# Down projections by a seven-product block algorithm, with VectorE making the low part of the four-block weight sum

## The chip, the cores and the metric

One core of a Trainium2 chip runs the program. The metric is the device time of one execution in microseconds (us). TensorE multiplies, VectorE, ScalarE and GpSimd do the elementwise work, and SyncE's queue issues most DMAs. A profile of one execution gives each instruction's start and duration.

## The reference, cut to what matters

Two decoder layers on 256 tokens with a model width of 2048: a sliding-window attention layer, then a forgetting-attention layer, each followed by this feed-forward network of inner width 5632 (float32 throughout):

```
def swiglu_ffn(h, w_gate_up, w_down):
    gu = h @ w_gate_up
    gate, up = gu[..., :D_FF], gu[..., D_FF:]
    return (jax.nn.silu(gate) * up) @ w_down

# around it, for each layer i
    h = rmsnorm(x, g[2])
    y = swiglu_ffn(h, ffn_w_gate_up[i], ffn_w_down[i])
    x = x + rmsnorm(y, g[3])
```

## The kernel before, in words

The program is a row of units. A unit is 16 weight tiles of 128 rows by 512 columns, each multiplied with two blocks of 128 tokens (t = 0 and 1), so 32 steps. To keep float32 precision on a cheaper format, each weight tile and each activation tile is split into a high part and a low part, and a step is three matmuls (`product`): high by high, high activation by low weight, low activation by high weight. So a unit is 96 matmuls of 128x512.

The feed-forward network of a layer has 11 groups of 512 inner columns. Before the change a group is three units: gate, up, and down. The gate unit is read by ScalarE with a SiLU into `h_sb` (L747); VectorE multiplies it with the up result (L1061), turns it in 32x32 blocks into `h_t` (L1087, 32 instructions a group), and it is split into `h_hi` (ScalarE, L752) and `h_lo` (VectorE, L1069). The down unit multiplies it with 16 tiles of `ffn_w_down` (4 inner blocks by 4 output chunks of 512), and VectorE adds each of the 8 results to `y_sb` (`add_y`, L1106).

Weight tiles come in pairs by DMA into `stage` (8 tiles). ScalarE rounds each to `ring_hi` (`round_tile`, L607 with a gain for gate and up, L605 for down), VectorE subtracts to get `ring_lo` (`rest_tile`, L817 and L815). The ring has 24 places; `tile_used` frees them, `lo_ready` lets TensorE go on. Each engine has one queue in program order, written out by hand as steps: in step s VectorE does what the tables name for it, then one tile. GpSimd does next to nothing in the feed-forward networks: it takes two square roots per norm (L1205) and loads gains (L1274). It is at work in the attention parts: rotary (L1220 to L1226) in the first, the bias (L1265 to L1267) and its DMAs in the second. Nine of the eleven groups of each layer run in a loop of three units.

Of the kernel before, what the change touches and what calls it, by code (L numbers as in the profile page):

```python
# [43 lines left out]
LT = LOOP_UNITS * UT  # L44
# [6 lines left out]
U_FOX = U_FFN[0] + 3 * FG  # L51
U_FOX_OUT = U_FOX + FOX_UNITS
U_FFN[1] = U_FOX_OUT + NC_D
U_END = U_FFN[1] + 3 * FG
# [45 lines left out]
HIDDEN_TURNED = {(1, 17): (0, 0), (1, 19): (0, 1), (2, 1): (1, 0), (2, 3): (1, 1)}  # L100
HIDDEN_HI = {(1, 25): 0, (2, 5): 1}
HIDDEN_LO = {(1, 23): 0, (2, 5): 1}
# [32 lines left out]
def step_order(s, first=False):  # L135

    if first:
        return s // 4 % 2, s // 8 * 4 + s % 4
    return s // UT, s % UT

# [22 lines left out]
def build(nc, x, positions, norm_gains, swa_w_in, swa_sinks, swa_w_out,  # L163
          fox_w_in, fox_b_f, fox_w_out, ffn_w_gate_up, ffn_w_down, out):
    with ExitStack() as ctx:
# [40 lines left out]
        arena = sb("arena", [P, 51 * 1024 // 4])  # L206
# [22 lines left out]
        diag = at("diag", 40 * KB, [P, P])  # L229
        ssq_end = at("ssq_end", 41 * KB, [P, NC_D + 1])  # L230
# [18 lines left out]
        x_ps = [bank[b] for b in (6, 7, 4, 5)]  # L249

# [20 lines left out]
        x_sum = sem("x_sum")  # L271
        x_squared, pre_mean, pre_rstd = sem("x_squared"), sem("pre_mean"), sem("pre_rstd")
# [12 lines left out]

        cum_dram = nc.dram_tensor("cum_scratch", (NH, SEQ), F32, kind="Internal").ap()
# [4 lines left out]
        def weights(u, i, pr):  # L291
# [16 lines left out]
            if u < U_FOX or u >= U_FFN[1]:  # L308
                layer = 0 if u < U_FOX else 1
                g, part = divmod(u - U_FFN[layer], 3)  # L310
                g = g + i
                if part < 2:
                    return cols(ffn_w_gate_up[layer], g * CH + part * D_FF)
# [14 lines left out]
        def gain_row(u):  # L328
# [37 lines left out]

        def whole_program(loop, unit):

            def looped(u, n):
                with loop(n) as i:  # L370
                    for part in range(LOOP_UNITS):
# [6 lines left out]
            straight(U_SWA, U_FFN[0] + 3)  # L378
            looped(U_FFN[0] + 3, FG - 2)
            straight(U_FOX - 3, U_FOX + 3)  # L380
            looped(U_FOX + 3, NG - 2)
            straight(U_FOX_OUT - 3, U_FFN[1] + 3)
            looped(U_FFN[1] + 3, FG - 2)
            straight(U_END - 3, U_END)

        def ffn_part(u):

            for layer in range(2):
                if U_FFN[layer] <= u < U_FFN[layer] + 3 * FG:
                    return (layer, *divmod(u - U_FFN[layer], 3))  # L390
            return None
# [133 lines left out]
        def _(sp):  # L525
# [1062 lines left out]
```

## Time and profile before

| | us |
|---|---|
| median of 2 runs | 2106.19 (2106.15 to 2106.24) |
| span of the profiled execution, first to last instruction | 2104.5 |
| TensorE busy | 2094.2 |
| TensorE weight loads busy (beside the matmuls) | 1718.9 |
| VectorE busy | 1615.4 |
| ScalarE busy | 1152.9 |
| GpSimd busy | 156.6 |

The page gives the time of the execution only as its span; what lies around it is the 1.7 us between the span and the median. Busy time counts a moment once even if two pipelined instructions overlap in it, so the mean duration of one matmul (0.39 us) is longer than the distance from one to the next.

### The profile page before, as it was taken

How to read it: one execution, taken by the hardware profiler on the slowest of the kernel's cores; microseconds unless marked ns; L12 is line 12 of the kernel's file. 1: busy time of each engine (PE TensorE's matmuls, PEld its weight loads, DVE VectorE, ACT ScalarE, POOL GpSimd, SP SyncE). 2: the span in 40 equal slices, each digit the busy share in tenths (PEclk: the TensorE clock that was granted, in tenths of full speed). 3: DMA queues.
4: the chain of work that ended last, by engine and by line, in shares of the span. 5: the costliest groups of instructions: out<-in, count | busy, mean ns of one | idle time of the engine just before them, and what ended most of it. 6: DMA issues, size and time to landing. Idle time of an engine off the chain costs nothing.

```text
span 2104.5 us, 32177 instructions
## 1 busy us (share of the span) xinstructions
PE 2094.2 (100%) x9603; PEld 1718.9 (82%) x9603; DVE 1615.4 (77%) x3299; ACT 1152.9 (55%) x2061; POOL 156.6 (7%) x311
## 2 busy tenths in 40 slices
PE   9999999999999999999999999999999999999998
PEld 7877888888888888888888887888888888888886
DVE  6798677887667776678898898577877668776686
ACT  7666565544455454555666555665544545445553
POOL 2110000000000000000152343000000000000000
PEclk9999999999999999999999999999999999999999
DMA  7699866665666655665687787756555665556662
GB/s 257 211 247 253 223 206 206 195 191 173 199 199 199 197 171 190 199 204 161 202 247 219 214 251 215 234 190 216 189 187 178 199 217 184 188 178 203 206 193 87
DMA packets 221564, 425.01 MB, mean 202 GB/s; under 512 B 15808, under 2 KB 25440, under 8 KB 220976
## 3 DMA queue, kind: packets, MB, share of 16 engines
q1 hardware_dynamic: 214528, 402.45, 61.6%
q0 software_dynamic: 6672, 21.31, 3.7%
q8 instruction: 37, 0.61, 0.1%
q10 hardware_dynamic: 288, 0.33, 0.1%
q14 instruction: 39, 0.32, 0.1%
HBM read 409.31 MB, written 14.71 MB: 201 GB/s over the span
## 4 chain that ended last, share of the span: by engine, by line
PE 97%; DMA 1%; issue 1%; SPq 1%; ACT 0%; POOL 0%; DVE 0%; POOLq 0%
PE bank L1338 31%; PE bank L1340 31%; PE bank L1339 31%; PE bank L1385 1%; PE bank L1410 1%; PE bank L1351 1%; DMA x_sb<-x 0%; DMA p_f<-first_scratch 0%; DMA stage<-swa_w_out 0%; PE bank L1368 0%; SPq L541 0%; SPq L566 0%; PE bank L1432 0%; PE bank L1429 0%; PE bank L1571 0%
## 5 line engine op out<-in xcount | busy, mean ns | idle before, releaser
L1338 PE MATMUL bank<-ring_hi,a_hi 128*128 128x512 f32 x2240 | 880.3, 393 | 0.5 <-DVE ring_lo L817 0.5
L1340 PE MATMUL bank<-ring_hi,a_lo 128*128 128x512 f32 x2240 | 873.1, 390 | 0.0
L1339 PE MATMUL bank<-ring_lo,a_hi 128*128 128x512 f32 x2240 | 872.8, 390 | 0.0
L607 ACT ACTIVATE ring_hi<-stage,g_t 128x512 fp32r<-128x512 f32 x992 | 661.2, 717 | 376.6 <-DMA stage<-ffn_w_gate_up 203.0
L817 DVE SCALAR_TENSOR_TENSOR ring_lo<-stage,g_t,ring_hi 128x512 fp32r<-128x512 f32 x992 | 708.5, 759 | 147.3 <-ACT ring_hi L607 144.9
L1338 PEld LDWEIGHTS bank<-ring_hi,a_hi 128*128 128x128 f32 x2240 | 420.9, 188 | 92.9 <-issue 5.9
L1340 PEld LDWEIGHTS bank<-ring_hi,a_lo 128*128 128x128 f32 x2240 | 420.8, 188 | 88.1
L1339 PEld LDWEIGHTS bank<-ring_lo,a_hi 128*128 128x128 f32 x2240 | 421.1, 188 | 84.7
L815 DVE TENSOR_TENSOR ring_lo<-stage,ring_hi 128x512 fp32r<-128x512 f32 x480 | 305.5, 687 | 139.9 <-ACT ring_hi L605 138.5
L605 ACT ACTIVATE ring_hi<-stage 128x512 fp32r<-128x512 f32 x480 | 278.4, 624 | 225.0 <-PE bank L1340 149.5
L1338 PE MATMUL bank<-ring_hi,h_hi 128*128 128x512 f32 x704 | 274.6, 390 | 0.0
L1340 PE MATMUL bank<-ring_hi,h_lo 128*128 128x512 f32 x704 | 274.2, 389 | 0.0
L1339 PE MATMUL bank<-ring_lo,h_hi 128*128 128x512 f32 x704 | 274.2, 389 | 0.0
L1087 DVE STREAM_TRANSPOSE h_t<-h_sb 32x128 f32<-32x128 f32 x672 | 203.5, 303 | 10.8
L1340 PEld LDWEIGHTS bank<-ring_hi,h_lo 128*128 128x128 f32 x704 | 132.2, 188 | 27.4
L1338 PEld LDWEIGHTS bank<-ring_hi,h_hi 128*128 128x128 f32 x704 | 132.3, 188 | 27.2
L1339 PEld LDWEIGHTS bank<-ring_lo,h_hi 128*128 128x128 f32 x704 | 132.3, 188 | 27.1
L1205 POOL TENSOR_TENSOR post_r<-post_ms,half_pow 128x1 f32<-128x1 f32 x8 | 7.6, 948 | 1491.6 <-DVE post_ms L844 1491.6
L1106 DVE TENSOR_TENSOR y_sb<-bank,y_sb 128x512 f32<-128x512 f32 x159 | 109.5, 688 | 11.6 <-PE bank L1340 10.8
L1061 DVE SCALAR_TENSOR_TENSOR h_sb<-bank,pre_r,h_sb 128x512 f32<-128x512 f32 x44 | 33.0, 749 | 108.8 <-PE bank L1340 108.8
L752 ACT ACTIVATE h_hi<-h_t 128x512 fp32r<-128x512 f32 x42 | 26.6, 633 | 125.7 <-DVE h_t L1087 125.7
L667 ACT ACTIVATE prob<-prob,neg_mx 128x129 f32<-128x129 f32 (+3 forms) x128 | 56.9, 447 | 39.6 <-DVE neg_mx L933 39.3
(148 smaller groups left out, 836.6 us busy)
## 6 DMA issues: line engine op xcount, KB each, us to landing
stage<-ffn_w_gate_up SPq DMA_DIRECT2D x352, 512.0 KB, 4.6
stage<-ffn_w_down SPq DMA_DIRECT2D x176, 512.0 KB, 5.5
stage<-fox_w_in SPq DMA_DIRECT2D x96, 512.0 KB, 4.7
stage<-swa_w_in SPq DMA_DIRECT2D x48, 512.0 KB, 4.7
stage<-swa_w_out SPq DMA_DIRECT2D x64, 256.0 KB, 6.2
stage<-fox_w_out SPq DMA_DIRECT2D x32, 512.0 KB, 5.5
first_scratch<-first_blocks SPq DMA_DIRECT2D x16, 384.0 KB, 5.4
p_f<-first_scratch SPq DMA_DIRECT2D x64, 96.0 KB, 3.9
```

The costliest lines, as they stand in the source:

```text
L605: nc.scalar.activation(ring_hi[:, n % RING, :], src, ACT.Identity).then_inc(hi_ready, 1)
L607: nc.scalar.activation(ring_hi[:, n % RING, :], src, ACT.Identity, scale=g_t[:, row * KT + j:row * KT + j + 1]).then_inc(hi_ready, 1)
L667: last = nc.scalar.activation(prob[:, b, cols], prob[:, b, cols], ACT.Exp, bias=neg_mx[:, j, t:t + 1], accum_out=den[:, j, t:t + 1])
L752: nc.scalar.activation(h_hi[:, :, tok(t)], hidden_transposed(g, t), ACT.Identity).then_inc(ht_hi, 1)
L815: nc.vector.tensor_tensor(lo, src, hi, ALU.subtract).then_inc(lo_ready, 1)
L817: nc.vector.scalar_tensor_tensor(out=lo, in0=src, scalar=g_t[:, row * KT + j:row * KT + j + 1], in1=hi, op0=ALU.mult, op1=ALU.subtract).th ...
L1061: nc.vector.scalar_tensor_tensor(out=h_sb[:, t, :], in0=main[2 + t][:, :], scalar=pre_r[:, t:t + 1], in1=h_sb[:, t, :], op0=ALU.mult, op1= ...
L1087: last = nc.vector.transpose(h_t[Q * b:Q * (b + 1), :, P * t + Q * a:P * t + Q * (a + 1)], src)
L1106: nc.vector.tensor_tensor(dst, main[n][:, :], dst, ALU.add).then_inc(y_added, 1)
L1338: nc.tensor.matmul(dst, hi_a, hi_w, start=start, stop=False)
L1339: nc.tensor.matmul(dst, hi_a, lo_w, start=False, stop=False)
L1340: return nc.tensor.matmul(dst, lo_a, hi_w, start=False, stop=stop)
```

## The change

The down projection of the first ten of a layer's eleven groups is no longer a unit of its own. Its 4 inner blocks by 4 output chunks are taken as two halves ("pairs", of 1024 output columns each). In a half the product is one of 2x2 blocks: rows are the two token blocks, the inner dimension is two times 256, the columns two chunks of 512. A seven-product algorithm (Strassen's, in Winograd's form) makes it from 7 block products where the plain one has 8. One block product is 6 matmuls (two inner blocks by three).

- A feed-forward group is now two units, gate and up (`FFN_LOOP_UNITS = 4` for two groups). While the units of group g run, the 7 products of each half of group g-1 are put between their steps (`down_pair`, at the steps of `PRODUCT_STEPS`). Gate and up take tiles in fours, alternating between the token blocks. The eleventh group keeps its plain down unit.
- The weights of a half come by 4 DMAs of 512 KB (`load_down`) into `down_w`, which lies over `x_sb`. So `x_sb` is written to DRAM at the start of each feed-forward network (`save_x`) and read back at its end (`load_x`), both on GpSimd's queue.
- GpSimd makes four sums of weight blocks of 128x1024 for each half (`sum_weights`): T1 = B11 + B12, T3 = B22 + B12, T2 = T1 + B22, T4 = T2 + B21, and, once a group, four sums of 128x256 of the turned hidden block (`sum_hidden`). It also makes the low part of T1 (`rest(T1)`).
- ScalarE rounds the seven 128x1024 weight operands of a half (`round_pair`). VectorE makes the low parts of the other six (`rest_pair`), T4's among them: the table `POOL_LO = (T1,)` sets which of them GpSimd makes. VectorE also does the low parts of the hidden sums (`sum_rests`) and adds the seven results to `y_sb` (`add_pair`).
- The turning into 32x32 blocks takes both token blocks at once: 16 instructions of 32x256 a group for 32 of 32x128.

```diff
-LT = LOOP_UNITS * UT
+FFN_LOOP_UNITS = 4
+FFN_UNITS = 2 * FG + 1
...
+B11, B21, T1, T2, B22, T3, T4 = range(NPROD)
+POOL_LO = (T1,)
+DVE_LO = tuple(k for k in range(NPROD) if k not in POOL_LO)
+SUMS = (T1, T3, T2, T4)
...
+            def rest_pair(u, i, k):
+
+                p = NPROD * pair_number(u) + k
+                dve.wait_ge(pair_hi, p + 1 + 4 * NPROD * i)
+                both = slice(PLACE["pair", p], PLACE["pair", p] + 2)
+                if k == B22:
+                    dve.wait_ge(sums_made, 4 * pair_number(u) + SUMS.index(T4) + 1 + 16 * i)
+                nc.vector.tensor_tensor(ring_lo[:, both, :], pair_source(k), ring_hi[:, both, :].bitcast(F32), ALU.subtract).then_inc(pair_lo, 1)
...
+                wait_loaded(0)
+                if q > 0:
+                    wait_rested(T4, q - 1)
+                nc.gpsimd.tensor_tensor(sums[0][:, :, :], b11, b12, ALU.add).then_inc(sums_made, 1)
+                wait_loaded(2)
+                pool.wait_ge(pair_lo, rested + DVE_LO.index(B11) + 1)
+                nc.gpsimd.tensor_tensor(sums[1][:, :, :], b22, b12, ALU.add).then_inc(sums_made, 1)
+                pool.wait_ge(sums_made, made + 1)
+                nc.gpsimd.tensor_tensor(sums[2][:, :, :], sums[0][:, :, :], b22, ALU.add).then_inc(sums_made, 1)
+                rest(T1)
+                pool.wait_ge(sums_made, made + 3)
+                wait_rested(T1, q)
+                nc.gpsimd.tensor_tensor(sums[0][:, :, :], sums[2][:, :, :], b21, ALU.add).then_inc(sums_made, 1)
+                if q % 2 == 0:
+                    sum_hidden(q, i)
+                rest(T4)
...
+                for r in range(2):
+                    if k in (0, 1, 6):
+                        first, t = ((0, 0), (2, 0), None, None, None, None, (2, 1))[k]
+                        a_h, a_l = h_hi[:, first + r, tok(t)], h_lo[:, first + r, tok(t)]
+                    else:
+                        n = (None, None, 0, 1, 2, 3, None)[k]
+                        a_h, a_l = s_hi[:, n, r, :], s_lo[:, n, r, :]
+                    slot = PLACE["pair", p] + r
+                    last = product(ps[:, :], a_h, a_l, ring_hi[:, slot, :], ring_lo[:, slot, :], k < 3 and r == 0, r == 1, True)
+                last.then_inc(pair_done, 1)
```

How the queues change. On GpSimd, before the change, the rows of the first feed-forward network are a load of gains and the norm's powers, and nothing else:

```order
L1205 TENSOR_TENSOR pre_r<-pre_ms,half_pow 128x1 x2
L1274 DMA g_b<-norm_gains 128x2048
L1205 TENSOR_TENSOR post_r<-post_ms,half_pow 128x1
L1298 DMA fg_raw<-fox_w_in 128x16x32
L1205 TENSOR_TENSOR post_r<-post_ms,half_pow 128x1
```

After it, at the same place, `x_sb` is saved and the first half of the first group follows (sums_67 holds T1 and later T4, sums_68 holds T3, sums_69 holds T2):

```order
L1562 DMA x_scratch<-x_sb 128x2x2048
L1596 TENSOR_TENSOR sums_67<-down_w 128x1024
L1599 TENSOR_TENSOR sums_68<-down_w 128x1024
L1601 TENSOR_TENSOR sums_69<-sums_67,down_w 128x1024
L1590 TENSOR_TENSOR ring_lo<-sums_67,ring_hi 128x1024
L1605 TENSOR_TENSOR sums_67<-sums_69,down_w 128x1024
L1616 TENSOR_TENSOR s_sb<-h_t 128x256
L1618 TENSOR_TENSOR s_sb<-s_sb,h_t 128x256
L1620 TENSOR_TENSOR s_sb<-s_sb,h_t 128x256
L1621 TENSOR_TENSOR s_sb<-h_t 128x256
```

Five instructions of 128x1024 for each half and four of 128x256 for each group have come in. On VectorE, in the first group's down unit before the change, one result is added between every two tiles:

```order
L1103 COPY y_sb<-bank 128x512
L817 SCALAR_TENSOR_TENSOR ring_lo<-stage,g_t,ring_hi 128x512 x2
L1103 COPY y_sb<-bank 128x512
L817 SCALAR_TENSOR_TENSOR ring_lo<-stage,g_t,ring_hi 128x512 x2
L1103 COPY y_sb<-bank 128x512
```

After it, in the unit that holds the first half's products, an instruction of twice the width stands in nearly every place between a tile and an addition (the second row of 128x1024 below, from sums_67, is the low part of T4):

```order
L1060 TENSOR_TENSOR s_lo<-s_sb,s_hi 128x512
L1024 SCALAR_TENSOR_TENSOR ring_lo<-stage,g_t,ring_hi 128x512
L1085 TENSOR_TENSOR y_sb<-bank,y_sb 128x512
L1034 TENSOR_TENSOR ring_lo<-sums_68,ring_hi 128x1024
L1024 SCALAR_TENSOR_TENSOR ring_lo<-stage,g_t,ring_hi 128x512
L1076 COPY y_sb<-bank 128x512
L1034 TENSOR_TENSOR ring_lo<-sums_67,ring_hi 128x1024
L1024 SCALAR_TENSOR_TENSOR ring_lo<-stage,g_t,ring_hi 128x512
L1074 TENSOR_SCALAR y_sb<-bank 128x512
L1034 TENSOR_TENSOR ring_lo<-down_w,ring_hi 128x1024
L1024 SCALAR_TENSOR_TENSOR ring_lo<-stage,g_t,ring_hi 128x512
```

What moved: the low parts of the down weights were 16 rows of 128x512 a group and are now 12 rows of 128x1024, spread between the gate and up tiles.

## Rows read from the trace of the kernel before

**Rows 1.** The page: busy time by engine, slices of the span, DMA.
```profile
PE 2094.2 (100%) x9603; PEld 1718.9 (82%) x9603; DVE 1615.4 (77%) x3299; ACT 1152.9 (55%) x2061; POOL 156.6 (7%) x311
...
PE   9999999999999999999999999999999999999998
...
PEclk9999999999999999999999999999999999999999
...
HBM read 409.31 MB, written 14.71 MB: 201 GB/s over the span
```
**Rows 2.** The page: the chain that ended last, by engine.
```profile
PE 97%; DMA 1%; issue 1%; SPq 1%; ACT 0%; POOL 0%; DVE 0%; POOLq 0%
```
**Rows 3.** Timeline of TensorE (start, duration): a down unit's first, the next unit's first.
```profile
703.17 0.39 PE L1338 MATMUL bank<-ring_hi,h_hi 128*128 128x512 f32 x1
703.40 0.39 PE L1339 MATMUL bank<-ring_lo,h_hi 128*128 128x512 f32 x1
...
724.94 0.39 PE L1338 MATMUL bank<-ring_hi,a_hi 128*128 128x512 f32 x1
```
**Rows 4.** Windows: stretch, its length, busy of PE, PEld, DVE, ACT, POOL, clock, DMA.
```profile
703.17:768.44 65.27, 65.27 (x289) 54.09 (x288) 48.97 (x93) 32.86 (x52) 0.00 (x0) 1.00 0.61 193
```
**Rows 5.** Groups of VectorE instructions in 703 to 768 us: busy, mean; idle before.
```profile
L817 DVE SCALAR_TENSOR_TENSOR ring_lo<-stage,g_t,ring_hi 128x512 fp32r<-128x512 f32 x32 | 22.5, 749 | 5.4 <-ACT ring_hi L607 5.4
L815 DVE TENSOR_TENSOR ring_lo<-stage,ring_hi 128x512 fp32r<-128x512 f32 x17 | 10.8, 687 | 4.6 <-ACT ring_hi L605 4.6
...
L1106 DVE TENSOR_TENSOR y_sb<-bank,y_sb 128x512 f32<-128x512 f32 x8 | 5.5, 690 | 0.5 <-PE bank L1340 0.5
L1061 DVE SCALAR_TENSOR_TENSOR h_sb<-bank,pre_r,h_sb 128x512 f32<-128x512 f32 x2 | 1.5, 748 | 5.3 <-PE bank L1340 5.3
```
**Rows 6.** Timeline of VectorE: stretches of equal instructions back to back.
```profile
1154.45 5.35 DVE L817 SCALAR_TENSOR_TENSOR ring_lo<-stage,g_t,ring_hi 128x512 fp32r<-128x512 f32 x8
1163.21 1.77 DVE L877 STREAM_TRANSPOSE k_t<-stg 32x256 f32<-32x256 f32 x4
748.21 4.30 DVE L815 TENSOR_TENSOR ring_lo<-stage,ring_hi 128x512 fp32r<-128x512 f32 x7 [3.86 <-ACT ring_hi L605]
703.91 0.74 DVE L1061 SCALAR_TENSOR_TENSOR h_sb<-bank,pre_r,h_sb 128x512 f32<-128x512 f32 x1
704.69 2.51 DVE L1087 STREAM_TRANSPOSE h_t<-h_sb 32x128 f32<-32x128 f32 x8
```
**Rows 7.** Groups of the whole span: the same operation at two widths.
```profile
L1106 DVE TENSOR_TENSOR y_sb<-bank,y_sb 128x512 f32<-128x512 f32 x159 | 109.5, 688 | 11.6 <-PE bank L1340 10.8
L1100 DVE TENSOR_TENSOR y_sb<-bank,y_sb 128x256 f32<-128x256 f32 x2 | 0.8, 419 | 0.3 <-PE bank L1340 0.3
```
**Rows 8.** Timeline of GpSimd in the attention parts.
```profile
80.75 0.32 POOL L1221 TENSOR_TENSOR rope_tmp<-stg,rope_s 128x64 f32<-128x64 f32 x1
81.14 0.96 POOL L1224 TENSOR_TENSOR stg<-stg,rope_c 128x128 f32<-128x128 f32 x1
1164.45 0.47 POOL L1265 TENSOR_TENSOR prob<-cum_b,mask 128x128 f32<-128x128 f32 x1
1171.34 0.47 POOL L1265 TENSOR_TENSOR prob<-cum_b,mask 128x128 f32<-128x128 f32 x1
1204.68 0.46 POOL L1267 TENSOR_TENSOR prob<-cum_b,mask 128x128 f32<-128x128 f32 x1
```
**Rows 9.** Timeline of VectorE beside them.
```profile
71.58 0.74 DVE L817 SCALAR_TENSOR_TENSOR ring_lo<-stage,g_t,ring_hi 128x512 fp32r<-128x512 f32 x1
81.70 0.96 DVE L817 SCALAR_TENSOR_TENSOR ring_lo<-stage,g_t,ring_hi 128x512 fp32r<-128x512 f32 x1
1171.33 1.27 DVE L817 SCALAR_TENSOR_TENSOR ring_lo<-stage,g_t,ring_hi 128x512 fp32r<-128x512 f32 x1
1195.16 0.17 DVE L933 TENSOR_SCALAR neg_mx<-row_mx 128x2 f32<-128x2 f32 x1
1204.70 0.47 DVE L933 TENSOR_SCALAR neg_mx<-row_mx 128x2 f32<-128x2 f32 x1
```
**Rows 10.** Groups of the whole span: ScalarE's rounding of a tile, with and without a gain.
```profile
L607 ACT ACTIVATE ring_hi<-stage,g_t 128x512 fp32r<-128x512 f32 x992 | 661.2, 717 | 376.6 <-DMA stage<-ffn_w_gate_up 203.0 <-PE bank L1340 107.6 <-DMA stage<-fox_w_in 55.5
L605 ACT ACTIVATE ring_hi<-stage 128x512 fp32r<-128x512 f32 x480 | 278.4, 624 | 225.0 <-PE bank L1340 149.5 <-DMA stage<-swa_w_out 35.2 <-DMA stage<-fox_w_out 23.5
```

More of the change, by code:

```diff
@@ L132, with ffn_index, pair_unit, pair_number @@
 OUT_GAIN = {84: (0, 0), 88: (1, 0), 92: (0, 1), 98: (1, 1), 102: (0, 2), 106: (1, 2)}
-def step_order(s, first=False):
-    if first:
+def ffn_index(u):
+    for layer in range(2):
+        if U_FFN[layer] <= u < U_FFN[layer] + FFN_UNITS:
+            return layer, u - U_FFN[layer]
+    return None
+def pair_unit(u):
+    f = ffn_index(u)
+    return f is not None and 2 <= f[1] < 2 * FG
+def pair_number(u):
+    layer, n = ffn_index(u)
+    return NP_LAYER * layer + n - 2
+def in_fours(u):
+    f = ffn_index(u)
+    return f is not None and 1 <= f[1] < 2 * FG - 1
@@ new lines, in tiles_rested @@
+def tiles_rested(u, s):
+    f = ffn_index(u)
+    uneven = f is not None and f[1] > 0
+    before = ffn_index(u - 1) if u else None
+    uneven_before = before is not None and 0 < before[1] < 2 * FG
+    if s == 0:
+        if u == 0:
+            return []
+        return tiles_rounded(u - 1, STEPS - 1) if uneven_before else [(u, UT - 1)]
+    if uneven and f[1] < 2 * FG:
+        return tiles_rounded(u, s - 1)
+    if uneven and s == 1:
+        return [(u, 15)]
+    return [(u + 1, s // 2 - 1)] if s % 2 == 0 else []
@@ new lines, in pairs_rounded, with ring_places @@
+def pairs_rounded(u, s):
+    f = ffn_index(u)
+    if f is None or f[1] == 0 or s not in PAIR_HI[f[1] % 2]:
+        return []
+    later, k = PAIR_HI[f[1] % 2][s]
+    return [(u + later, k)] if pair_unit(u + later) else []
+def ring_places():
+    place, before, last = {}, {}, {}
+    n = 0
+    for u in range(U_END):
+        f = ffn_index(u)
+        fixed = f is not None and f[1] >= 2
+        if fixed and f[1] == 2:
+            first = n % RING
+        for j in range(UT):
+            slot = (first + j) % RING if fixed else n % RING
+            if not fixed:
+                n += 1
+            place[u, j] = slot
+            before[u, j] = last.get(slot)
+            last[slot] = ("tile", u * UT + j)
+        if pair_unit(u):
+            for k in range(NPROD):
+                p = NPROD * pair_number(u) + k
+                slot = (first + UT + 2 * (p % 4)) % RING
+                place["pair", p] = slot
+                before["pair", p] = last[slot + 1]
+                last[slot] = last[slot + 1] = ("pair", p)
+        if fixed and f[1] == 2 * FG:
+            n = first + UT
+    return place, before
@@ L229, in build @@
         diag = at("diag", 40 * KB, [P, P])
+        sums = [at(f"sums{n}", (32 + 4 * n) * KB, [P, 2, CH]) for n in range(3)]
+        s_hi = at("s_hi", 44 * KB, [P, 4, 2, P], F32R)
+        s_lo = at("s_lo", 48 * KB, [P, 4, 2, P], F32R)
+        s_sb = at("s_sb", 8 * KB, [P, 4, 2, P])
+        x_base = x_sb.manual_sbuf_range[0] if x_sb.manual_sbuf_range else nc.lookup_mloc(x_sb).addr
+        down_w = nc.alloc_sbuf_tensor_at("down_w", [P, 8, CH], F32, offset=x_base)
         ssq_end = at("ssq_end", 41 * KB, [P, NC_D + 1])
@@ new lines, in hidden_rests, with sum_rests @@
+            def hidden_rests(u, i):
+                layer, g, _ = ffn_part(u)
+                dve.wait_ge(ht_hi, hidden_split(layer, g - 1, 0) + 2 * i)
+                nc.vector.tensor_tensor(h_lo[:, :, :], h_t[:, :, :], h_hi[:, :, :].bitcast(F32), ALU.subtract).then_inc(ht_lo, 1)
+            def sum_rests(u, i, half):
+                dve.wait_ge(s_hi_made, pair_number(u) + half + 1 + 4 * i)
+                part = slice(2 * half, 2 * half + 2)
+                nc.vector.tensor_tensor(s_lo[:, part], s_sb[:, part], s_hi[:, part].bitcast(F32), ALU.subtract).then_inc(s_lo_made, 1)
@@ L1483, in accumulator @@
                         if g > 0:
[L1484 removed]
+                            pe.wait_ge((gate_read, hidden)[part], 2 * (f - 1) + t + 1 + 4 * i)
                         elif part == 0:
```

372 lines of the change are left out of this document (292 added, 80 removed).

## The prediction

> **What bounds the kernel now.** I read the page's busy shares first: TensorE is busy for all of the span, at full clock in every slice, VectorE for 77% [rows 1]. The chain that ended last is 97% TensorE [rows 2], so a matmul saved is time saved, as long as no other engine takes over. The price of a matmul is its distance to the next, not its duration: a down unit starts at 703.17 and the next unit at 724.94, 96 matmuls in 21.77 us, 0.227 us each [rows 3]. One feed-forward group, three such units, lasts 65.27 us; in it VectorE is busy for 48.97 us, ScalarE for 32.86 us and GpSimd not at all [rows 4]. VectorE has 16 us to spare, which is little beside what the change gives it.
>
> **TensorE.** A group's down projection goes from 96 matmuls to 2 halves x 7 products x 6 = 84. With 10 groups in each of 2 layers that is 20 x 12 = 240 matmuls, 240 x 0.227 = 54.4 us. By TensorE alone a group would last 65.3 - 2.7 = 62.6 us, and the kernel 2106.2 - 54.4 = 2051.8 us. (The sum is made against the profiled execution, whose span is 1.7 us below the median; I add the same 1.7 us behind every sum by starting from 2106.2.)
>
> **VectorE's own work.** I again take distances, of equal instructions back to back [rows 6]: a gate or up tile (5.35 - 0.75)/7 = 0.66 us, a plain 128x512 subtraction (4.30 - 0.69)/6 = 0.60 us, a narrow block transpose 2.51/8 = 0.31 us, a wide one 1.77/4 = 0.44 us, the gate multiply 704.69 - 703.91 = 0.78 us. By these a group before costs 32 x 0.66 + 16 x 0.60 + 8 x 0.60 (additions) + 32 x 0.31 + 2 x 0.78 + 2 x 0.60 = about 48 us, which agrees with the 48.97 us. No row shows a 128x1024 subtraction. At least it is one of 128x512 (0.60 us), at most two (1.20 us). From 256 to 512 columns the same operation grows from 419 to 688 ns [rows 7], 1.05 ns a column, so I take 0.60 + 0.54 = 1.14 us. A group afterwards: 32 tiles 21.1, 12 wide low parts 13.7, 14 additions 8.4, 16 wide transposes 7.1, gate multiplies 1.6, `h_lo` 1.1, `s_lo` 2 x 0.6 = 1.2: together 54.2 us. That is under 62.6, and alone it would let TensorE stay the bound. The two low parts of T4 that stand here and not on GpSimd are 2.3 us of it.
>
> **ScalarE** has 14 roundings of 128x1024 for 16 of 128x512. A narrow one takes 0.62 us [rows 10], so a wide one is between that and 1.25 us; even at 1.25 us the group costs 32.9 + 14 x 1.25 - 16 x 0.62 = 40 us of 62, hidden. I cost it at nothing. The DMAs move the same weight bytes at about 200 GB/s [rows 1]; `x_sb` is saved and read back twice, 2.1 MB each time, 10 us each at that rate. The load is issued when the last half's low parts are made, in the middle of the last up unit, and is first needed at step 17 of the last down unit, more than 25 us later; the save has the unit and a half of gate and up before SyncE's queue reaches the first `load_down`, behind which the tiles of gate and up queue. I cost them at nothing; if that cover is gone it is 10 us at each of four places.
>
> **GpSimd, and what it does to VectorE.** This decides. Per group GpSimd gets ten additions or subtractions of 128x1024 and four of 128x256. The undisturbed rows are 0.32 us at 64 columns and 0.47 us at 128 [rows 8]: 0.15 us for 64 columns, 2.27 ns a column. So 1024 columns are 0.47 + 2.03 = 2.5 us and 256 are 0.75 us, together 28 us of a group. The bound above is eight times the 128-column row, 3.8 us; the bound below is the slope of VectorE, 0.47 + 0.94 = 1.4 us. I keep 2.5, from two rows of the same engine and operation (at 3.8 a group would gain another 14 us, at 1.4 lose 12; the lower end is in the first rival, the upper in the last). In throughput 28 us would fit into 62. But the trace shows that it isn't laid beside VectorE's work. The tile at 71.58 takes 0.74 us with no addition of GpSimd at its start; the one at 1171.33 takes 1.27 us, and GpSimd's addition at 1171.34 lasts 0.47 us: the whole of it has been added. The one at 81.70 takes 0.96 us beside GpSimd's at 81.14, which itself takes 0.96 us for 0.47, since it had to wait for the tile before. A tiny VectorE instruction at 1204.70 takes 0.47 us for 0.17, until GpSimd's of 1204.68 ends [rows 8, 9]. Whoever comes second waits for the other's end. The block transposes at 1163.21 keep their 0.44 us with GpSimd's addition at 1164.45 in the middle of them [rows 6, 8], so work with one input in SBUF is spared.
>
> The Trainium skill's page "SBUF — State Buffer", section "Who interferes with whom", has this as a rule: a VectorE instruction with two SBUF inputs and a GpSimd instruction that reads SBUF share a read port, and the later one is blocked for the whole of the other. By that rule the blocking lasts the full length of a wide GpSimd addition, which no row here can show, since the widest of them is 128 columns. The same skill's "GPSIMD Engine Reference", section "Performance versus the Vector engine", gives 4497 ns at 2048 columns, by which 1024 would be an estimated 2.25 us and the sum below about 50 us smaller.
>
> What is exposed: VectorE's tiles, wide low parts, `h_lo` and `s_lo` (21.1 + 13.7 + 1.1 + 1.2 = 37.1 us) read two SBUF inputs. Additions, transposes and gate multiplies (8.4 + 7.1 + 1.6 = 17.1 us) are spared. With GpSimd's 28 that makes 65.1 us that cannot overlap, already more than TensorE's 62.6. To reach even that, all 17.1 us of spared work would have to lie under GpSimd's. It does not: in VectorE's queue a single addition of 0.60 us stands between exposed instructions, so a GpSimd addition of 2.5 us covers one of them at best. Half of the ten long ones covering one is 3 us; another 5 us I allow for time in which VectorE would wait for ScalarE or TensorE anyway (15 us a group now, [rows 5], most of which the fuller queue eats up). So VectorE needs 54.2 + 28 - 8 = 74.2 us a group. TensorE waits for it through `lo_ready`, `pair_lo` and `pair_added`; ScalarE waits behind TensorE for ring places. The sum: (74.2 - 65.3) x 20 = +178 us, 2106.2 + 178 = 2284 us. VectorE is then what is late next, and GpSimd, at 28 us plus its own waits, is not.
>
> **The rivals.**
> - TensorE stays the bound, faster: GpSimd's long additions do not hold up VectorE for their whole length (or cost near the lower bound: 10 x 1.4 + 4 x 0.6 = 16.4, less 8, makes 62.6 us, just the point at which TensorE decides). For it speaks that each engine alone fits into 62.6 us and that no row shows a wide addition; against it that every short collision in rows 8 and 9 costs the full remainder. 2052 us, up to 2060 with some exposed DMA. Chance 0.12.
> - The collisions are real but nearly all of the spared work and of VectorE's idle time lies under them: 54.2 + 28 - 17.1 = 65.1 us, 2102 us; between 64 and 67 us a group, 2080 to 2140 us. For it: GpSimd starts when VectorE's work allows, and its dependences could fall into a rhythm. Against it: the order of the queues. Chance 0.14, most of it within 2% of before.
> - Worse than forecast: nothing is covered, and VectorE's in-order waits for GpSimd's sums come on top: 54.2 + 28 = 82.2 us, 2444 us, and more still if a wide addition is nearer to 3.8 us. GpSimd's chain T1, T3, T2, low part of T1, T4 is five long additions, 12.5 us plus waits for VectorE, in a unit of some 35 us, so it should keep up. Chance 0.06.
> - The change doesn't save the matmuls: excluded, they are counted in the code.
>
> **How the numbers follow.** The forecast, VectorE bound by collisions, has 0.68 and spans about 69 to 79 us a group, 2180 to 2380 us. The range takes in a part of the second rival: 2110 to 2380 us; it leaves out the first (0.12) and the last (0.06). A measurement of this kernel can tell about 2% from no change, which is 42 us. Faster by over 2% needs less than 63.2 us a group: 0.12. Within 2%: 0.12. Slower by over 2%: 0.68 + 0.06 + 0.02 = 0.76.
>
> **What the profile would show.** Right: TensorE busy well under 90% of the feed-forward stretches, its idle time ended by VectorE's `ring_lo`; gate and up tiles of VectorE with a mean clearly over 749 ns in the feed-forward, near 1.1 us; additions from PSUM unchanged near 690 ns; GpSimd's 128x1024 instructions at 2.5 us or longer; VectorE busy near all of the time. 240 fewer matmuls show in the counts in any case. Wrong: a VectorE tile mean near 750 ns with GpSimd busy beside it (then the first rival), GpSimd instructions far from 2.5 us, a lower granted clock while TensorE waits (which rows of before cannot price), or waits ended by `x_scratch` DMAs.

## The result, and the profile after

The changed kernel takes 2318.53 us (2317.94 to 2319.11, two runs) for 2106.19 before: 1.101 times as long, 95% interval 1.099 to 1.103. The forecast was 2284 us, slower. The changed kernel's profiled execution has a span of 2317.4 us. Of the page, the busy shares, VectorE's slices, the granted clock by slices and the chain that ended last, beside [rows 1, 2]:

```profile
PE 2124.6 (92%) x9363; PEld 1716.7 (74%) x9363; DVE 2065.6 (89%) x3039; ACT 1261.9 (54%) x2041; POOL 811.0 (35%) x595
...
DVE  7796779999999999998898887779999999999997
...
PEclk9999989999999999989999999999999999999989
...
PE 59%; DVE 23%; issue 11%; DMA 3%; ACT 3%; POOL 0%; DVEq 0%; SPq 0%; ACTq 0%; POOLq 0%
```

The matmuls fell by the counted 240 (9603 to 9363), but the chain is no longer TensorE's alone: VectorE has 23% of it and is full in every feed-forward slice. One group, read in windows as in [rows 4] (length, then busy time of PE, PEld, DVE, ACT, POOL, the clock, DMA):

```profile
700.45:775.49 75.04, 66.69 (x278) 53.95 (x277) 71.38 (x79) 38.28 (x51) 32.66 (x14) 0.95 0.52 168
```

75.0 us for 65.3 (over the 18 groups behind each layer's first, the mean is 74.9). VectorE works in 71.4 of them; its own work was put at 54.2. The 17 us between stand in its instructions' lengths. VectorE's groups in that window (busy, mean; idle before), beside [rows 5]:

```profile
L1024 DVE SCALAR_TENSOR_TENSOR ring_lo<-stage,g_t,ring_hi 128x512 fp32r<-128x512 f32 x32 | 34.5, 1096 | 0.0
L1034 DVE TENSOR_TENSOR ring_lo<-down_w,ring_hi 128x1024 fp32r<-128x1024 f32 x6 | 12.4, 2069 | 0.5 <-ACT ring_hi L793 0.5
L1034 DVE TENSOR_TENSOR ring_lo<-sums,ring_hi 128x1024 fp32r<-128x1024 f32 x6 | 7.3, 1215 | 0.2 <-ACT ring_hi L793 0.2
L1046 DVE STREAM_TRANSPOSE h_t<-h_sb 32x256 f32<-32x256 f32 x16 | 7.0, 436 | 0.4
L1085 DVE TENSOR_TENSOR y_sb<-bank,y_sb 128x512 f32<-128x512 f32 x10 | 6.8, 681 | 0.5 <-PE bank L1696 0.4
```

The tiles of gate and up went from 749 to 1096 ns. Additions that read a PSUM bank (681) kept their length, and so did the block transposes (436), but these prove nothing: GpSimd has no instruction beside any of them in this window, since it waits for their result (`s_sb` waits for `h_t`, 14.6 us). Of the wide low parts, those from `sums` take 1215 ns and those from `down_w`, the same operation at the same width, 2069. Their places in the queue tell them apart: the ones from `down_w` stand beside GpSimd's chain. That chain in the same window:

```profile
L1601 POOL TENSOR_TENSOR sums<-sums,down_w 128x1024 f32<-128x1024 f32 x2 | 6.2, 3090 | 0.0
L1599 POOL TENSOR_TENSOR sums<-down_w 128x1024 f32<-128x1024 f32 x2 | 5.7, 2853 | 2.9 <-DVE ring_lo L1034 2.9
L1596 POOL TENSOR_TENSOR sums<-down_w 128x1024 f32<-128x1024 f32 x2 | 5.7, 2852 | 24.1 <-DVE ring_lo L1034 24.1
L1590 POOL TENSOR_TENSOR ring_lo<-sums,ring_hi 128x1024 fp32r<-128x1024 f32 x2 | 5.6, 2795 | 0.5 <-ACT ring_hi L793 0.5
L1605 POOL TENSOR_TENSOR sums<-sums,down_w 128x1024 f32<-128x1024 f32 x2 | 5.4, 2710 | 0.2
```

How the two meet is in the timeline (start, length), first VectorE, then GpSimd, and last a GpSimd addition with no reading VectorE instruction under way, in the first group:

```profile
727.10 0.74 DVE L1024 SCALAR_TENSOR_TENSOR ring_lo<-stage,g_t,ring_hi 128x512 fp32r<-128x512 f32 x1
727.77 0.68 DVE L1085 TENSOR_TENSOR y_sb<-bank,y_sb 128x512 f32<-128x512 f32 x1
728.37 2.83 DVE L1034 TENSOR_TENSOR ring_lo<-down_w,ring_hi 128x1024 fp32r<-128x1024 f32 x1
731.12 2.84 DVE L1024 SCALAR_TENSOR_TENSOR ring_lo<-stage,g_t,ring_hi 128x512 fp32r<-128x512 f32 x1
```
```profile
727.26 2.85 POOL L1599 TENSOR_TENSOR sums<-down_w 128x1024 f32<-128x1024 f32 x1 [1.17 <-DVE ring_lo L1034]
730.07 3.34 POOL L1601 TENSOR_TENSOR sums<-sums,down_w 128x1024 f32<-128x1024 f32 x1
...
301.05 2.39 POOL L1596 TENSOR_TENSOR sums<-down_w 128x1024 f32<-128x1024 f32 x1 [14.82 <-DMA down_w<-ffn_w_down]
```

GpSimd's addition is called at 727.26, waits for the rest of VectorE's tile of 727.10 (2.85 us for 2.39) and ends at 730.11. VectorE's low part is called at 728.37, waits until about 730.0 and then runs its 1.2 us; GpSimd's next one, called at 730.07, waits for that (3.34 for 2.39); VectorE's tile at 731.12 waits for it in turn, 2.84 us for 0.74. The addition from PSUM at 727.77 ran beside GpSimd at its normal 0.68.

TensorE's waits in that window (in total, times, longest):

```profile
PE bank L1694 <- DVE y_sb L1083: 5.4, 2, 2.9
...
PE bank L1694 <- DVE h_lo L1054: 3.0, 1, 3.0
```

And its matmuls after the second kind of pause:

```profile
712.12 0.79 PE L1694 MATMUL bank<-ring_hi,h_hi 128*128 128x512 f32 x1 [3.00 <-DVE h_lo L1054]
712.71 0.63 PE L1695 MATMUL bank<-ring_lo,h_hi 128*128 128x512 f32 x1
713.13 0.63 PE L1696 MATMUL bank<-ring_hi,h_lo 128*128 128x512 f32 x1
713.56 0.63 PE L1694 MATMUL bank<-ring_hi,h_hi 128*128 128x512 f32 x1
```

They lie 0.43 us apart for 0.227 [rows 3]: the clock was granted at its lower level (1.2 GHz, where it was 2.4). This happens twice in a group and lasts about 3.4 us each time: at once after the 3.0 us pause for `h_lo`, and 1.6 us after the end of the longer pause for `y_sb` (2.9 us, matmuls again from 734.61, slow from 736.20 to 739.5). After the shorter one (2.4 us) the matmuls keep their 0.23 us. It is the 0.95 of the window.

### The profile page after: what moved, and what is told of

Same layout as the page of the kernel before. It is cut to its first block, busy times and chain, and to the rows that moved or that the text cites. A ratio compares the mean times of both kernels' runs of the same rounds, so it can differ in the third digit from the quotient of the medians.

```text
span 2317.4 us, 31986 instructions
## 1 busy us (share of the span) xinstructions
PE 2124.6 (92%) x9363; PEld 1716.7 (74%) x9363; DVE 2065.6 (89%) x3039; ACT 1261.9 (54%) x2041; POOL 811.0 (35%) x595
## 4 chain that ended last, share of the span: by engine, by line
PE 59%; DVE 23%; issue 11%; DMA 3%; ACT 3%; POOL 0%; DVEq 0%; SPq 0%; ACTq 0%; POOLq 0%
PE bank L1694 19%; PE bank L1695 18%; PE bank L1696 18%; DVE ring_lo L1024 8%; DVE h_t L1046 6%; DVE ring_lo L1034 3%; DMA stage<-ffn_w_gate_up 2%; DVE h_lo L1054 1%; DVE y_sb L1083 1%; PE bank L1741 1%; PE bank L1766 1%; ACT h_hi L802 1%; ACT ring_hi L793 1%; DVE h_sb L1363 1%; ACT ring_hi L780 1%
## 5 line engine op out<-in xcount | busy, mean ns | idle before, releaser
L1024 DVE SCALAR_TENSOR_TENSOR ring_lo<-stage,g_t,ring_hi 128x512 fp32r<-128x512 f32 x992 | 948.1, 982 | 62.9 <-ACT ring_hi L780 61.1
L793 ACT ACTIVATE ring_hi<-sums 128x1024 fp32r<-128x1024 f32 x160 | 169.8, 1061 | 282.8 <-PE bank L1696 281.9
L1694 PE MATMUL bank<-ring_hi,h_hi 128*128 128x512 f32 x304 | 137.7, 453 | 181.6 <-DVE y_sb L1083 112.0
L1596 POOL TENSOR_TENSOR sums<-down_w 128x1024 f32<-128x1024 f32 x40 | 112.5, 2812 | 481.8 <-DVE ring_lo L1034 444.1
L1034 DVE TENSOR_TENSOR ring_lo<-down_w,ring_hi 128x1024 fp32r<-128x1024 f32 x120 | 249.0, 2075 | 9.0 <-ACT ring_hi L793 8.5
L1034 DVE TENSOR_TENSOR ring_lo<-sums,ring_hi 128x1024 fp32r<-128x1024 f32 x120 | 145.9, 1216 | 5.6 <-ACT ring_hi L793 5.5
L1046 DVE STREAM_TRANSPOSE h_t<-h_sb 32x256 f32<-32x256 f32 x320 | 139.6, 436 | 7.0
L1022 DVE TENSOR_TENSOR ring_lo<-stage,ring_hi 128x512 fp32r<-128x512 f32 x160 | 104.6, 687 | 41.1 <-ACT ring_hi L778 40.9
L778 ACT ACTIVATE ring_hi<-stage 128x512 fp32r<-128x512 f32 x160 | 95.1, 624 | 81.2 <-DMA stage<-swa_w_out 34.2
L1599 POOL TENSOR_TENSOR sums<-down_w 128x1024 f32<-128x1024 f32 x40 | 113.2, 2830 | 61.9 <-DVE ring_lo L1034 59.4
L1696 PE MATMUL bank<-ring_hi,h_lo 128*128 128x512 f32 x304 | 131.4, 432 | 0.0
```

Source lines behind the costliest of these rows:

```text
L793: nc.scalar.activation(ring_hi[:, PLACE["pair", p]:PLACE["pair", p] + 2, :], pair_source(k), ACT.Identity).then_inc(pair_hi, 1)
L1022: nc.vector.tensor_tensor(lo, src, hi, ALU.subtract).then_inc(lo_ready, 1)
L1024: nc.vector.scalar_tensor_tensor(out=lo, in0=src, scalar=g_t[:, row * KT + j:row * KT + j + 1], in1=hi, op0=ALU.mult, op1=ALU.subtract).th ...
L1034: nc.vector.tensor_tensor(ring_lo[:, both, :], pair_source(k), ring_hi[:, both, :].bitcast(F32), ALU.subtract).then_inc(pair_lo, 1)
L1046: last = nc.vector.transpose(dst, src)
L1596: nc.gpsimd.tensor_tensor(sums[0][:, :, :], b11, b12, ALU.add).then_inc(sums_made, 1)
```

## The experiments

Theory A is that of the prediction: GpSimd's instructions that read SBUF stop VectorE's instructions with two SBUF inputs for their whole length, so the two engines' amounts add up. Its rival B: VectorE simply has too much work at the lengths it has now, and what GpSimd does has no part in it. A third, C: it isn't the blocking but GpSimd's results that come late. Each number below is one run, unless rounds are named; seven runs of the kernel before lay within 0.1% of each other.

### GpSimd's instructions made narrow

The changed kernel with GpSimd's five wide instructions of each half cut to 32 columns, except in each layer's first half; the sums are then incomplete.

```diff
+                w = dst.shape[-1] if q % NP_LAYER == 0 else 16
+                last = nc.gpsimd.tensor_tensor(dst[:, :, 0:w], x[:, :, 0:w], y[:, :, 0:w], op)
```

> GpSimd's five 128x1024 instructions of a half are cut to 128x32, with all their waits kept (the first half of each layer stays full, and the rest of the sums keeps old numbers, so this part of the computation is left out). Theory A (GpSimd's reading blocks VectorE's instructions with two SBUF inputs): the blocking of about 16 us a group shrinks to 2 to 3 us, VectorE needs about 57 us, TensorE is the bound again with 62.6 us a group: 2050 to 2080 us, VectorE's gate and up tiles back at 750 to 780 ns. Theory B (VectorE's own larger work and its in-order waits for TensorE): GpSimd doesn't matter, 2290 to 2320 us. Theory C (the sums arrive late) expects the same as A; the next run tells them apart.

### GpSimd busy, but only writing

The same, and behind each narrow instruction GpSimd fills the rest of its output with constants by 12 memsets, so it stays busy longer and its results come later, without reading; the sums are left out as above.

```diff
+                if q % NP_LAYER:
+                    for r, n in ((0, 62), (1, 124)):
+                        for first in range(16, CH, n):
+                            part = dst[:, r, first:first + n]
+                            last = nc.gpsimd.memset(part.bitcast(F32) if op == ALU.subtract else part, 0.01)
```

> As in the run before, but behind each narrow instruction GpSimd fills the rest of the same output with 12 memsets, which write and read nothing, so that it is busy for about 2 us again for each sum and its results come as late as in the changed kernel (sums are left out of the computation). Theory A, with only reads blocking: 2050 to 2090 us, VectorE's tiles near 750 to 800 ns. Theory A with writes blocking as well: 2250 us or more. Theory C (GpSimd's lateness, not the blocking): 2290 to 2320 us, as changed.

Measured: 2113.07 us narrow and 2111.21 us writing only, beside 2104.43 before; groups of 64.2 us in both. VectorE's tiles and low parts of the first, from 640 to 701 us:

```profile
L1024 DVE SCALAR_TENSOR_TENSOR ring_lo<-stage,g_t,ring_hi 128x512 fp32r<-128x512 f32 x31 | 23.5, 774 | 0.9 <-ACT ring_hi L780 0.8
L1034 DVE TENSOR_TENSOR ring_lo<-sums,ring_hi 128x1024 fp32r<-128x1024 f32 x6 | 7.3, 1215 | 0.0
L1034 DVE TENSOR_TENSOR ring_lo<-down_w,ring_hi 128x1024 fp32r<-128x1024 f32 x6 | 7.3, 1214 | 0.0
```

and of the second, in the same stretch, some of GpSimd's memsets, VectorE's low parts, and the window from 640 to 785 us (GpSimd busy for 46 us of 145):

```profile
L1578 POOL MEMSET sums<- 128x62 f32 x64 | 5.9, 147 | 0.0
L1578 POOL MEMSET sums<- 128x124 f32 x32 | 5.0, 199 | 0.0
...
L1034 DVE TENSOR_TENSOR ring_lo<-down_w,ring_hi 128x1024 fp32r<-128x1024 f32 x6 | 7.3, 1213 | 0.0
```
```profile
640.00:785.00 145.00, 141.81 (x624) 116.46 (x622) 126.17 (x184) 81.96 (x110) 46.12 (x288) 1.00 0.61 192
```

With no wide read, 205 us are gone, the low parts from `down_w` are back at 1214 ns and the tiles at 774. B falls: VectorE has the same instructions in all three kernels. With 12.3 us of writes a group more (46.1 us for 18.4 in the window), the lengths are the same to 2 ns: writing stops nobody. The writes put back half of the 24.5 us that GpSimd lost by the narrow instructions (8.1 us a group busy, for 32.7 in the changed kernel and 20.4 here), and this half of its lateness cost nothing. C is thereby unlikely; in full it was not tested by this run. Both times lie above A's ranges, which ended at 2080 and 2090 us: above TensorE's 2051.8 us there remain 1.6 us a group, 1.4 of them a wait of TensorE for `h_lo`, and the long first groups (below).

### Who makes the low parts

T4's low part goes to GpSimd too, or T1's comes to VectorE:

```diff
-POOL_LO = (T1,)
+POOL_LO = (T1, T4)
```

> The table POOL_LO becomes (T1, T4): GpSimd makes the low part of the four-block sum too, two more 128x1024 instructions a group there, two fewer on VectorE. Theory A: VectorE loses 2.3 us of work and gains about 2 x 1.6 to 2.2 us of blocking: 2336 to 2360 us. Theory B (VectorE's own work is what counts): 2318 - 20 x 2.3 = 2273 us.

```diff
-POOL_LO = (T1,)
+POOL_LO = ()
```

> The table POOL_LO becomes (): VectorE makes the low part of T1 too, GpSimd keeps the sums. The step of two low parts a group from VectorE to GpSimd cost 2345 - 2319 = 27 us, so theory A expects the same with the other sign: VectorE gains 2.3 us of work and loses more than that in blocking, about 2291 us (2276 to 2300). Theory B, VectorE's own work alone: 2318 + 46 = 2364 us.

Measured: 2345.26 us and 2289.99 us (before: 2104.43 and 2105.58), with 2318.53 between; both in A's ranges. Each of the two steps moves 40 wide low parts (two in each of 20 groups) from VectorE to GpSimd and costs 27 to 29 us, 0.7 us each. VectorE is rid of 1.14 us and loses 1.8 us. B, by which giving VectorE less must help, falls by its sign. The tiles' lengths show where it goes (from 640 to 785 us, T1's and T4's low part on GpSimd, then neither; with T1's alone 1096 ns):

```profile
L1024 DVE SCALAR_TENSOR_TENSOR ring_lo<-stage,g_t,ring_hi 128x512 fp32r<-128x512 f32 x62 | 75.1, 1228 | 0.7 <-ACT ring_hi L780 0.7
L1024 DVE SCALAR_TENSOR_TENSOR ring_lo<-stage,g_t,ring_hi 128x512 fp32r<-128x512 f32 x63 | 60.1, 969 | 0.1
```

Each step adds about 4.1 us to a group's 32 tiles, 2.0 to 2.1 us for one wide instruction of GpSimd.

### All of GpSimd's work on VectorE

```diff
+SUM_STEPS = ({26: (1, T1), 30: (1, T2), 6: (0, T3), 10: (0, T4)}, {20: (1, T1), 28: (1, T2), 2: (0, T3), 4: (0, T4)})
...
+                nc.vector.tensor_tensor(dst[:, :, :], x, y, ALU.add).then_inc(sums_made, 1)
...
+                    if ffn and part < 2 and s in SUM_STEPS[part]:
+                        later, k = SUM_STEPS[part][s]
+                        if pair_unit(u + later):
+                            sum_weights(u + later, i, k)
```

> GpSimd does nothing in the pair work: VectorE makes the eight weight sums, the four hidden sums and the low part of T1 as well, 12.7 us more work a group on the engine that is the bound. Theory A: its blocking of 16.7 us goes, 54.2 + 12.7 = 66.9 us, with 1 to 2 us of waits 68 to 69 us a group: 2150 to 2190 us, tiles at 750 ns, no GpSimd rows. Theory B: 75 + 12.7 us a group, 2570 us.

Measured: 2218.99 us, 100 less than the changed kernel though VectorE has about 12.7 us a group more to do. B, with 2570 us, falls. A's range ended at 2190 us and was missed by 29 us: the groups behind a layer's first last 69 to 74 us, 70.3 on average. The window, and TensorE's wait in it:

```profile
640.00:785.00 145.00, 132.72 (x569) 108.96 (x568) 138.17 (x191) 78.46 (x106) 0.00 (x0) 0.96 0.55 177
```
```profile
PE bank L1671 <- DVE h_lo L1086: 12.3, 2, 7.7
```

VectorE is busy for 138 of 145 us, 67.0 a group, the amount that it was given (66.9); it idles for 3.3 us a group, and TensorE waits for `h_lo`, behind 16 block transposes, 7.7 us at the longest. VectorE is the bound here by its own amount.

### The hidden block turned by TensorE

On top of the last: 8 TensorE transposes a group into two PSUM tiles that the norm uses, and 2 copies by ScalarE, for VectorE's 16 block transposes.

```diff
-TURNED_STEPS = (2, 4, 6, 8)
+TURNED_STEPS = (4, 8)
...
+                last = nc.scalar.activation(h_t[:, :, tok(t)], xt_ps[t][:, :].rearrange("p (k m) -> p k m", k=4), ACT.Identity)
...
+                    last = nc.tensor.transpose(xt_ps[t][:, k * P:(k + 1) * P], h_sb[:, t, k * P:(k + 1) * P], ident[:, :])
```

> On top of the run with all sums on VectorE (2219 us): the hidden block is turned by 8 TensorE transposes a group into two free banks and copied out by ScalarE, so VectorE loses its 16 transposes (7.1 us a group) and GpSimd still does nothing. VectorE's work is 66.9 - 7.1 = 59.8 us a group, under TensorE's 62.6 plus about 1 us of transposes. If VectorE's amount of work is what is left of the excess: 64 to 65 us a group, with the 27 us at the starts 2105 to 2127 us. If it is the order of steps (a wait in each group that stays): 2140 us or more.

Measured once 2077.5 us, and then in three rounds:

> The kernel with all sums on VectorE and the turning on TensorE once more, timed against the kernel before in three rounds for an interval: 2077.5 us, a ratio of 0.986 to 0.987.

2078.06 us (2076.77 to 2080.04) beside 2105.61: 0.987, interval 0.985 to 0.989. This version beats both kernels, the one before by 1.3%. It is also 28 us under the lower end of its own forecast (2105 to 2127), which had kept the long first groups and groups of 64 to 65 us: the first went with the turning (below), and a group lasts 63.5. Its page and the window from 640 to 785 us:

```profile
PE 2060.0 (99%) x9523; PEld 1686.8 (81%) x9523; DVE 1835.5 (88%) x2999; ACT 1280.3 (62%) x2081; POOL 159.3 (8%) x315
...
PE 92%; DVE 3%; DMA 2%; issue 1%; SPq 1%; ACT 1%; POOL 0%; POOLq 0%; DVEq 0%; ACTq 0%
```
```profile
640.00:785.00 145.00, 145.00 (x648) 120.04 (x648) 135.69 (x175) 89.21 (x121) 0.00 (x0) 1.00 0.61 196
```

TensorE does not stop once in 145 us, at full clock, with groups of 63.5 us. So the saved matmuls are real; they show as soon as VectorE (135.7 of 145, 59.4 a group) is under TensorE.

The same turning in the changed kernel, whose sums stay on GpSimd:

> The changed kernel, GpSimd's sums and their blocking as they are, but the hidden block is turned by TensorE and copied out by ScalarE: 7.1 us a group less on VectorE. If VectorE is the bound, each of its microseconds is worth one: 75.0 - 7.1 = 67.9 us a group and the first groups shorter too, 2318 - 142 - 10 = 2166 us (2155 to 2185). If GpSimd's chain of sums were the bound, nearly nothing: 2300 to 2318 us.

Measured: 2265.3 us, a miss by 99 us. VectorE lost 7.1 us of work a group and the group only 2.3 (72.7 us on average). The window, and VectorE's wait before `h_lo`:

```profile
640.00:785.00 145.00, 132.70 (x570) 108.10 (x569) 129.19 (x127) 78.58 (x107) 66.08 (x29) 0.96 0.53 174
```
```profile
DVE h_lo L1054 <- ACT h_hi L814: 11.1, 2, 5.7
```

VectorE's idle time grew from 3.7 to 7.9 us a group, and nearly all of the growth is this one wait: 5.5 us a group for `h_hi`, 1.2 in the changed kernel. The path to `h_lo` now leads through two other queues: the second multiply, TensorE's transposes (the second token block's), ScalarE's copy and rounding, and `h_lo`:

```profile
756.92 0.74 DVE L1361 SCALAR_TENSOR_TENSOR h_sb<-bank,pre_r,h_sb 128x512 f32<-128x512 f32 x1
761.98 0.60 PE L1807 MATMUL bank<-ident,h_sb 128*128 128x128 f32 x4
762.61 0.60 ACT L803 ACTIVATE h_t<-bank 128x512 f32<-128x512 f32 x1 [2.61 <-PE bank L1807]
763.24 1.06 ACT L814 ACTIVATE h_hi<-h_t 128x1024 fp32r<-128x1024 f32 x1
764.34 1.59 DVE L1054 TENSOR_TENSOR h_lo<-h_t,h_hi 128x1024 fp32r<-128x1024 f32 x1 [5.36 <-ACT h_hi L814]
```

From the end of the multiply to the start of `h_lo` it is 6.7 us here (7.1 the other time in the window), of which 4.3 pass until TensorE reaches its transposes in its own queue. It is 6.5 us in the version with all sums on VectorE too (696.83 to 703.35), where GpSimd does nothing. But there VectorE has a weight sum and the four hidden sums to do meanwhile and idles only 1.5 us; here its queue has two tiles. GpSimd's chains, two of some 16 us a group, still hold VectorE up as before (tiles 1105 ns, low parts from `down_w` 2133):

```profile
705.69 2.84 POOL L1594 TENSOR_TENSOR sums<-down_w 128x1024 f32<-128x1024 f32 x1 [10.35 <-DVE ring_lo L1048]
709.70 2.85 POOL L1597 TENSOR_TENSOR sums<-down_w 128x1024 f32<-128x1024 f32 x1 [1.16 <-DVE ring_lo L1048]
...
718.71 2.75 POOL L1603 TENSOR_TENSOR sums<-sums,down_w 128x1024 f32<-128x1024 f32 x1
```

The miss refutes the step "a microsecond taken from VectorE is one taken from the group": the work was traded for a path that VectorE has to wait out. That it would have gained the full 7.1 us with other work put into that wait is my reading; no run moved only the order of VectorE's queue.

### Three suspects that cost nothing, or little

From ScalarE's first silu of a group to the next group's, a layer's first group lasts 66.6 us (the second layer's 65.1). Its interval holds only one half's products, 234 matmuls, which TensorE would do in 53.1 us; in the kernel before, with a down unit in it, it is 60.9 us. ScalarE waits 11.9 us for `ffn_w_gate_up` there, behind the save of `x_sb`. The save by token blocks, as soon as each is ready:

```diff
+            def save_x(b, t):
+                pool.wait_ge(x_new, 8 * (b - 1) + 4 * t + 4)
+                pool.dma_start(x_dram[:, t, :], x_sb[:, t, :]).then_inc(x_saved, 16)
```

> The changed kernel with one edit: x_sb is saved in two halves as soon as each is final, and SyncE's queue, not GpSimd, waits for the last readers of x_sb. In the changed kernel and in both runs with a quiet GpSimd the first group of a layer is 13.5 us too long (66.6 us from its first to the next group's first read of a gate bank, for 53.1). If the save, behind which the gate and up tiles queue, makes that: 2318 - 27 = 2291 us. If something else in the first group makes it (the missing products, VectorE's order): 2318 us.

Measured: 2317.08 us; the wait fell to 3.1 us and the first group still lasts 66.3. The save was not on the path. What the traces show in its place is one wait of TensorE for `h_lo` in that group, 11.8 us with the late save and 11.8 us with the early one:

```profile
PE bank L1694 <- DVE h_lo L1054: 11.8, 1, 11.8
```

It is 9.8 us with all sums on VectorE (first groups of 63.3 and 62.3 us) and gone with the turning on TensorE as well (55.0 and 53.6 us). So the long first groups go with VectorE's way to `h_lo`. Why it is so long there, no run takes apart. Put into the version with the turning:

> The run before and the early save together: 27 us less than that run if the save makes the long first groups, so 2078 to 2100 us, faster than the kernel before the change by up to 1.3%. If not, the same as that run.

2076.74 us beside 2077.5: nothing, where 27 us were expected if the save made the long first groups. Without the early save that version's first interval is 55.0 us already.

Sixteen small matmuls of the identity ahead of the wait for `h_lo` keep TensorE busy there:

```diff
+                if k == 0 and half == 0:
+                    for _ in range(16):
+                        nc.tensor.matmul(first_ps[0][:, 0:P], ident[:, :], ident[:, :], start=True, stop=True, skip_group_check=True)
```

> The changed kernel, with 16 matmuls of 128x128 on the identity in front of TensorE's wait for h_lo, once a group, into the bank that the next product starts afresh. In the changed kernel the granted clock falls to half twice a group, for 3.4 us each, after TensorE's pauses before h_lo and before a y_sb addition, and the matmuls then lie 0.43 us apart for 0.23. If this is part of why a group takes 75.0 us, the first of the two stretches goes and the group loses up to 1.6 us: 2286 us. If VectorE (71.4 us busy of 75.0) sets the pace and TensorE catches up anyway: 2312 to 2322 us.

Measured: 2326.3 us (before: 2105.61), 8 more, mean clock 0.966 for 0.963; neither of the two forecasts (2286, or 2312 to 2322) has it. The 16 matmuls (32 records, two for each) last 3.5 us from 710.42 to 713.91, a little longer than the pause they fill, and a group grows by 0.2 to 0.3 us. Behind them the matmuls lie 0.23 us apart. But now the shorter pause for `y_sb`, after which the changed kernel's matmuls kept their speed, is followed by slow ones:

```profile
693.03 0.50 PE L1694 MATMUL bank<-ring_hi,h_hi 128*128 128x512 f32 x1 [2.42 <-DVE y_sb L1083]
...
693.68 0.63 PE L1696 MATMUL bank<-ring_hi,h_lo 128*128 128x512 f32 x1
694.11 0.63 PE L1694 MATMUL bank<-ring_hi,h_hi 128*128 128x512 f32 x1
...
710.42 3.73 PE L1792 MATMUL bank<-ident 128*128 128x128 f32 x32
713.91 0.48 PE L1694 MATMUL bank<-ring_hi,h_hi 128*128 128x512 f32 x1
714.23 0.40 PE L1695 MATMUL bank<-ring_lo,h_hi 128*128 128x512 f32 x1
714.46 0.39 PE L1696 MATMUL bank<-ring_hi,h_lo 128*128 128x512 f32 x1
```

There are two slow stretches a group as before, one of them at another place. So this is no clean test of what the clock costs; it shows that a filler there doesn't pay.

## Why the prediction was right, point by point

- **TensorE, right.** 240 matmuls fewer, and the version with the turning shows a group of 63.5 us where TensorE is the bound: 62.6 predicted, and 8 transposes on top.
- **VectorE's own work, right.** 54.2 us a group were summed. Of the measured 71.4, the hold-ups read from the lengths are 32 x (1.096 - 0.742) = 11.3 us in the tiles (0.742 is their length with GpSimd idle, all sums on VectorE), 6 x (2.069 - 1.215) = 5.1 in the low parts from `down_w` and 0.3 in `h_lo` (1.48 for 1.22), 16.7 in all; 54.7 are left. A wide low part is 1.21 us long and 1.14 from start to start (with the narrow run 305.03 to 306.17), as interpolated from [rows 7].
- **GpSimd, right.** 2.5 us for a wide addition from two narrow rows [rows 8]: 2.39 undisturbed, 2.7 to 3.1 with its own waits. The Trainium skill's "GPSIMD Engine Reference", section "Performance versus the Vector engine", gave an estimated 2.25 us; the measured 2.39 lies between the two, 0.14 above it and 0.11 below the 2.5.
- **The blocking, right.** For the whole of a wide instruction, in both directions, sparing PSUM readers: the timeline at 727 us shows all of it, the narrow run removes it. This is the rule of the Trainium skill's "SBUF — State Buffer", section "Who interferes with whom", and the trace agrees at 1024 columns as at 128. The writing-only run shows that it is reading that blocks. That transposes are spared rests on the attention parts alone (32x256 in 432 to 439 ns beside GpSimd's additions, before and after); in the feed-forward none of them met GpSimd, so of the 17.1 us that I called spared their 7.1 us could cover nothing.
- **The covered share, mis-sized, with two errors that cancel.** I let 8 of GpSimd's 28 us be covered, so 20 exposed. Exposed are 16.7, and VectorE idles for 3.7 more: 54.7 + 16.7 + 3.7 = 75.1 us for the predicted 74.2. The 5 us of it that I gave to "time in which VectorE would wait anyway" assumed those waits away; the in-order waits remained. That the sum came within 1 us of a group is therefore in part luck.
- **Who ends TensorE's idle time, wrong.** I named `ring_lo`. It is `y_sb`, the additions that free a bank, and `h_lo` behind the transposes. In the window they are 5.4 and 3.0 of its 8.35 idle us. Both stand in VectorE's queue behind delayed tiles, so the sum holds, but whoever looked for `ring_lo` would have missed the place that the turning then relieved.
- **Clock, unpriced.** It was named as what no row of before can price. Two half-clock stretches of 3.4 us a group lose 1.6 us of matmuls each. That TensorE would otherwise only wait longer for VectorE is argued; no run shows it. They also spoil a sign: TensorE is busy for 66.7 of 75.0 us, 89%, and not "well under 90%", since slow matmuls count as busy for longer.
- **ScalarE, nearly right**: 38.3 us of 75, under the 40 allowed; VectorE waited for it for 1.9 us a group, 1.2 of them for `h_hi`. **`x_sb`, right in worth only**: the wait that its cover should have hidden is there, 11.9 us, but taking most of it away gained 1.5 us.
- **A layer's edges, missing.** My flat 8.9 us for each of 20 groups is, above TensorE's own time, 20 x 11.6 = 232 us. The traces have, above TensorE's own 2051.8 us: 18 x (75.0 - 62.6) = 223 us for the groups behind a layer's first, 13.5 + 12.0 for the two first ones (66.6 and 65.1 for 53.1), and about 2 x 6 for the stretches from the eleventh group's gate on, which hold the last half's products (7.2 us longer than in the version with the turning, both times). That is 2313 us, against 2318.5. Of the 34 us between forecast and result some 15 come from the group's size (12.4 for 11.6 us), some 14 from the edges (37.5 us for 2 x 11.6), and about 5 stay unexplained.

What stays open is the share of the in-order waits. Without GpSimd VectorE still idles 3.3 us a group, with the turning taken off and GpSimd's reads kept 7.9 us. No simple sum of amounts gave 2219 or 2265.

## What to carry over

Work on GpSimd with SBUF inputs isn't beside VectorE's but in its queue: price it in VectorE's time, here about 1.8 us for a low part that VectorE makes in 1.14, and give it to GpSimd only if VectorE meanwhile reads PSUM, transposes or idles. When an algorithm saves work on the bound, add up first the next engine's amount and its hold-ups; here the saving of 54 us needed VectorE under 63 us a group. Where engines wait for each other in order, a term taken off one of them is worth at most itself; 7.1 us taken off VectorE gave 2.3, because its result then came by a path of 6.7 us through two other queues, with nothing in VectorE's own queue to fill the wait.

## What the runs showed of the hardware

- GpSimd memsets in SBUF don't delay VectorE's two-input instructions at all (1213 for 1214 ns, with GpSimd busy for a third of the time).
- An fp32 addition of 128x1024 from SBUF takes 2.39 us on GpSimd and 1.22 us on VectorE.
- After two of a group's three pauses (3.0 and 2.9 us, not 2.4) TensorE's matmuls lay 0.43 us apart for about 3.4 us, after 0.227 ahead of them. With matmuls of the identity put into the 3.0 us pause they were slow after both others, the one of 2.4 us included, and the mean clock stayed nearly the same (0.966 for 0.963).
